# Putting a norm's token factors on all partitions: two GpSimd transfers through DRAM in place of diagonals and a product

## What is computed

```python
def _rmsnorm(x, g):
    r = lax.rsqrt(jnp.mean(xf * xf, axis=-1, keepdims=True) + EPS)
    return (xf * r).astype(x.dtype) * g

def _even_mixer(h, w_in, a_conv, b_conv, b_conv_bias, b_ln_g, b_ln_b, w_out):
    p = h @ w_in                      # 2048 -> 7168
    a_x, a_b, a_c, a_z, b_val, b_gate, b_z = jnp.split(p, 7, axis=-1)
    ya = a_b * _causal_dwconv(a_c * a_x, a_conv)          # 3 taps
    yb = b_val * jax.nn.sigmoid(b_gate)
    yb = _causal_dwconv(yb, b_conv) + b_conv_bias         # 31 taps
    yb = jax.nn.silu(_layernorm(yb, b_ln_g, b_ln_b))
    u = jnp.concatenate([ya * jax.nn.silu(a_z), yb * jax.nn.silu(b_z)], axis=-1)
    return u @ w_out

x = x + _rmsnorm(_even_mixer(_rmsnorm(x, e_norm_pre), ...), e_norm_post)
```

## Time and profile before

| | |
|---|---|
| median of 3 runs | 1347.89 us (1346.43 to 1349.7) |
| the profiled execution's own time | 1346.3 us |
| its span in the trace | 1344.5 us |
| TensorE (PE) busy | 99% of the span |
| TensorE weight loads (PEld), beside its matmuls | 82% |
| VectorE (DVE) busy | 65% |
| ScalarE (ACT) busy | 33% |
| GpSimd (POOL) busy | 7% |
| TensorE's granted clock | 0.998 of full speed |

### The profile page before, as it was taken

The page is one execution under the profiler, slowest core; times in us unless marked ns, Lnnn a source line. Parts: engine busy times, 40 slices in busy tenths (PEclk is TensorE's granted clock), DMA queues, the critical chain, the costliest instruction groups (busy, mean ns, idle before and its releaser), DMA issues.

```text
span 1344.5 us, 14691 instructions
## 1 busy us (share of the span) xinstructions
PE 1326.9 (99%) x6054; PEld 1104.8 (82%) x6054; DVE 874.3 (65%) x827; ACT 440.7 (33%) x436; POOL 96.9 (7%) x90
## 2 busy tenths in 40 slices
PE   8999999999999999999999899999999999999997
PEld 7888888888888888888888799888888888788886
DVE  6499999999846544536955984444522222499788
ACT  6421212221222121234555552222222223345452
POOL 0000000000009400000000100000000001400001
PEclk9999999999999999999999999999999999999999
DMA  9723333343368888753666554333343333364157
GB/s 319 218 63 94 102 106 105 94 125 94 102 179 274 250 258 250 251 188 107 241 258 233 163 161 125 96 95 95 100 113 94 94 94 95 125 219 157 43 208 251
DMA packets 229967, 209.50 MB, mean 156 GB/s; under 512 B 3616, under 2 KB 192160, under 8 KB 224928
## 3 DMA queue, kind: packets, MB, share of 16 engines
q1 hardware_dynamic: 225552, 203.61, 48.6%
q10 hardware_dynamic: 4368, 5.24, 1.2%
HBM read 187.87 MB, written 20.97 MB: 155 GB/s over the span
## 4 chain that ended last, share of the span: by engine, by line
PE 90%; DVE 5%; DMA 2%; ACT 1%; issue 1%; DVEq 0%; POOL 0%; SPq 0%; ACTq 0%
PE bank L705 30%; PE bank L709 30%; PE bank L707 30%; DVE w_lo L1490 1%; DMA scratch<-o_out 1%; DVE rows L1652 1%; ACT w_hi L1038 1%; DVE h_lo L1321 1%; DMA raw<-o_in 1%; DVE scratch L1522 1%; DVE rows L1569 0%; ACT junk L1190 0%; DVE scratch L1663 0%; DVE w_lo L1301 0%; DMA rows<-x_t 0%
## 5 line engine op out<-in xcount | busy, mean ns | idle before, releaser
L705 PE MATMUL bank<-h_hi,w_hi 128*128 128x512 f32 (+1 forms) x1536 | 585.6, 381 | 3.1 <-DVE w_lo L1343 1.6
L709 PE MATMUL bank<-h_hi,w_lo 128*128 128x512 f32 (+1 forms) x1536 | 584.0, 380 | 0.0
L707 PE MATMUL bank<-h_lo,w_hi 128*128 128x512 f32 (+1 forms) x1536 | 584.0, 380 | 0.0
L705 PEld LDWEIGHTS bank<-h_hi,w_hi 128*128 128x128 f32 x1536 | 288.8, 188 | 59.2 <-issue 4.0
L707 PEld LDWEIGHTS bank<-h_lo,w_hi 128*128 128x128 f32 x1536 | 288.8, 188 | 55.6 <-issue 0.7
L709 PEld LDWEIGHTS bank<-h_hi,w_lo 128*128 128x128 f32 x1536 | 288.8, 188 | 54.9
L1301 DVE TENSOR_TENSOR w_lo<-raw,w_hi 128x2048 fp32r<-128x2048 f32 x88 | 205.4, 2334 | 54.2 <-ACT w_hi L938 53.1
L1377 DVE SCALAR_TENSOR_TENSOR rows<-shifted,vecs,rows 128x512 f32<-128x512 f32 x256 | 198.8, 779 | 15.0 <-ACT rows L1000 7.6
L938 ACT ACTIVATE w_hi<-raw 128x2048 fp32r<-128x2048 f32 x88 | 167.9, 1910 | 87.3 <-PE bank L709 75.3
L705 PE MATMUL bank<-w_hi,h_hi 128*128 128x512 f32 x448 | 174.8, 390 | 0.6 <-DVE rows L1561 0.6
L709 PE MATMUL bank<-w_hi,h_lo 128*128 128x512 f32 x448 | 174.3, 389 | 0.0
(11 more groups left out here) (116 smaller groups left out, 718.3 us busy)
## 6 DMA issues: line engine op xcount, KB each, us to landing
raw<-e_in SPq DMA_DIRECT2D x52, 1024.0 KB, 5.7
raw<-o_in SPq DMA_DIRECT2D x32, 1024.0 KB, 6.1
scratch<-e_out SPq DMA_DIRECT2D x17, 1024.0 KB, 7.4
spare<-e_out SPq DMA_DIRECT2D x12, 1024.0 KB, 7.8
spare<-o_out SPq DMA_DIRECT2D x12, 1024.0 KB, 6.7
scratch<-o_out SPq DMA_DIRECT2D x10, 1024.0 KB, 5.1
e_sums<-scratch SPq DMA_DIRECT2D x8, 1024.0 KB, 5.1
spare<-e_sums SPq DMA_DIRECT2D x7, 1024.0 KB, 6.1
```

What stands on the lines that cost most here:

```text
L705: nc.tensor.matmul(dst, w[0], m[0], start=first, stop=False, skip_group_check=goes_on)
L707: nc.tensor.matmul(dst, w[0], m[1], start=False, stop=False, skip_group_check=goes_on)
L709: return nc.tensor.matmul(dst, w[1], m[0], start=False, stop=last, skip_group_check=goes_on)
```

## The change

The factors no longer pass TensorE. After each of the two powers GpSimd waits for it, writes the 128x4 tile `token_power` into a row of 512 words in DRAM (`rstd_rows[n]`, one word per token, so 512 places of 4 bytes), waits until that has landed, and reads the row back to all 128 partitions (2 KB each) straight into `x_rstd` or `ln_rstd`. VectorE waits for the second transfer where it waited for TensorE's product. Both sets of diagonals, both products of ones with diagonals and both copies from PSUM are gone; the square stays. The wait of step 1's last slab for `x_rstd_ready` goes with them, since bank 3 is not used for the factors any more.

```diff
--- before.py
+++ after.py
@@ -41,7 +41,6 @@
 KT = D // P
 QUARTER = KT // 4
 HALF = T // 2
-R_BANK = 3
 W_A = D // 2
 CB = W_A // P
 CONV_A, CONV_B = 3, 31
@@ -145,7 +144,7 @@
         scratch = sb("scratch", [P, KT * T])
         shifted_at = free_from[0]
         shifted = sb("shifted", [P, 3, PAD + T])
-        diagonals = sb("diagonals", [P, TT, P])
+        shifted_rest = sb("shifted_rest", [P, T])
         vecs = sb("vecs", [P, NVEC])
         ident = sb("ident", [P, P])
         ones = sb("ones", [P, P])
@@ -176,7 +175,6 @@
                   "b1": scratch[:, 3 * SLAB:], "b4": spare4[:, :]}
         buffers = [{**shared, "b2": spare2[n][:, :], "b3": spare3[n][:, :]} for n in range(2)]
         sum_buffer = (shared["b1"], shared["b4"])
-        ln_diagonals = scratch[:, 6 * T:7 * T].rearrange("p (t c) -> p t c", t=TT)
         gain_post = (shared["b1"], shared["c0"])
         gain_next = shared["c2"]
         x_resid = (shared["b0"], shared["b4"], shared["c3"], shared["b0"])
@@ -194,6 +192,8 @@
 
 
         x_mid = nc.dram_tensor("x_mid", [T, D], F32, kind="Internal").ap()
+        rstd_rows = [nc.dram_tensor(f"rstd_row{n}", [1, T], F32, kind="Internal").ap()
+                     for n in range(2)]
         e_sums = nc.dram_tensor("e_sums", [3, 4, P, SLAB], F32, kind="Internal").ap()
 
 
@@ -208,8 +208,9 @@
         x_squared = sem("x_squared")
         x_var_ready = sem("x_var_ready")
         x_power_ready = sem("x_power_ready")
-        x_spread = sem("x_spread")
         x_rstd_ready = sem("x_rstd_ready")
+        rstd_stored = sem("rstd_stored")
+        rstd_spread = sem("rstd_spread")
         sig_ready = sem("sig_ready")
         glu_ready = sem("glu_ready")
         silu_ready = sem("silu_ready")
@@ -239,7 +240,6 @@
         csum_ready = sem("csum_ready")
         vsum_ready = sem("vsum_ready")
         ln_rstd_ready = sem("ln_rstd_ready")
-        diagonals_ready = sem("diagonals_ready")
         ln_scaled = sem("ln_scaled")
         ln_silu = sem("ln_silu")
         gated = sem("gated")
@@ -295,7 +295,7 @@
         def uses4(b, part, n=0):
 
 
-            mid = 1 if b == 7 else 2
+            mid = 2 if b in (4, 5) else 1
             return {"stat": 1, "mid": mid, "map": mid + TT}[part] + n
 
         def first_bank(c):
@@ -652,6 +652,17 @@
             nc.gpsimd.tensor_tensor(token_power[:, :], token_var[:, :],
                                     minus_half[:, 0:1].to_broadcast([P, TT]),
                                     ALU.pow).then_inc(x_power_ready, 1)
+            pool.wait_ge(x_power_ready, 1)
+
+            def spread(n, dst):
+
+                pool.dma_start(rstd_rows[n].rearrange("a (t p) -> p (a t)", p=P),
+                               token_power[:, :], allow_slow_non_contiguous=True)\
+                    .then_inc(rstd_stored, 16)
+                pool.wait_ge(rstd_stored, 16 * (n + 1))
+                pool.dma_start(dst, rstd_rows[n].to_broadcast([P, T])).then_inc(rstd_spread, 16)
+
+            spread(0, x_rstd)
 
             def powers(first, count):
 
@@ -682,6 +693,8 @@
             nc.gpsimd.tensor_tensor(token_power[:, :], token_var[:, :],
                                     minus_half[:, 0:1].to_broadcast([P, TT]),
                                     ALU.pow).then_inc(ln_rstd_ready, 1)
+            pool.wait_ge(ln_rstd_ready, 1)
+            spread(1, ln_rstd)
 
             powers(MID, 2 * TT)
             pool.wait_ge(normed, 2 * TT)
@@ -716,14 +729,12 @@
             def operand(k, first=0, width=T):
                 return h_hi[:, k, first:first + width], h_lo[:, k, first:first + width]
 
-            def feature_major(step, moving, order=range(KT), used_at=None, before=None):
+            def feature_major(step, moving, order=range(KT), used_at=None):
 
                 for q in range(SLOTS):
                     pe.wait_ge(lo_ready, step * SLOTS + (q + 1))
                     pe.wait_ge(bank_free[q], step + 1)
                     for i, k in enumerate(order):
-                        if before is not None:
-                            before(q, i)
                         last = product(bank[q][:, :], weights(q, k, P), moving(k),
                                        i == 0, i == KT - 1)
                         if i == used_at and q == SLOTS - 1:
@@ -778,16 +789,7 @@
                 for k in range(KT):
                     first_product(q, k)
 
-            def x_spread_out(q, k):
-
-                if (q, k) == (0, QUARTER):
-                    pe.wait_ge(diagonals_ready, TT)
-                    nc.tensor.matmul(bank[R_BANK][:, :], ones[:, :], diagonals[:, :, :],
-                                     start=True, stop=True).then_inc(x_spread, 1)
-                elif (q, k) == (R_BANK, 0):
-                    pe.wait_ge(x_rstd_ready, 1)
-
-            feature_major(1, operand, before=x_spread_out)
+            feature_major(1, operand)
             with pe.Fori(2, E1A) as i:
                 feature_major(i, operand)
             with pe.Fori(E1A, E1A + 1) as i:
@@ -805,11 +807,6 @@
                                         ones[:, 0:1], start=True, stop=True)
             last.then_inc(stat_ready, 1)
             feature_major(E1A + E1B - 1, operand)
-            pe.wait_ge(diagonals_ready, 2 * TT)
-            pe.wait_ge(bank_free[6], uses4(6, "stat") + 1)
-            nc.tensor.matmul(bank[6][:, :], ones[:, :], ln_diagonals,
-                             start=True, stop=True)\
-                .then_inc(stat_ready, 1)
             with pe.Fori(E1A + E1B, E1 - 1) as i:
                 feature_major(i, operand)
             feature_major(E1 - 1, operand, [*range(2 * QUARTER, 3 * QUARTER),
@@ -1322,12 +1319,6 @@
                         h_halves[1][at], bank[4 + j][:, :].rearrange("p (k c) -> p k c", c=P),
                         f32(h_halves[0][at]), ALU.subtract).then_inc(bank_free[4 + j], 1)
 
-            def make_diagonals(dst):
-                for t in range(TT):
-                    nc.vector.tensor_scalar(dst[:, t, :], ident[:, :],
-                                            token_power[:, t:t + 1], None, ALU.mult)\
-                        .then_inc(diagonals_ready, 1)
-
             def x_rest(k):
 
                 dve.wait_ge(x_hi_ready, k + 1)
@@ -1359,12 +1350,9 @@
             nc.vector.tensor_scalar(token_var[:, :], x_sums[:, :], 1.0 / D, EPS,
                                     ALU.mult, ALU.add).then_inc(x_var_ready, 1)
             split_ahead(0, 2)
-            dve.wait_ge(x_power_ready, 1)
             dve.wait_ge(consts_set, 6)
-            make_diagonals(diagonals)
             split_ahead(0, 3)
-            dve.wait_ge(x_spread, 1)
-            link(nc.vector.tensor_copy(x_rstd, bank[R_BANK][:, :]))
+            dve.wait_ge(rstd_spread, 16)
             nc.vector.tensor_tensor(x_rstd2, x_rstd, x_rstd, ALU.mult).then_inc(x_rstd_ready, 1)
             dve.wait_ge(x_rstd_ready, 1)
 
@@ -1465,15 +1453,10 @@
                         dve.wait_ge(stat_ready, 2)
                         nc.vector.tensor_scalar(token_var[:, :], bank[5][:, 0:TT], 1.0 / W_A, EPS,
                                                 ALU.mult, ALU.add).then_inc(bank_free[5], 1)
-                    if i == E1B - 1 and q == 1:
-                        dve.wait_ge(ln_rstd_ready, 1)
-                        make_diagonals(ln_diagonals)
             finish(CB - 1, (CB - 1) % 2, tile(CB - 1))
 
 
-            dve.wait_ge(stat_ready, 3)
-            nc.vector.tensor_copy(ln_rstd, bank[6][:, :]).then_inc(bank_free[6], 1)
-            dve.wait_ge(bank_free[6], uses4(6, "stat") + 2)
+            dve.wait_ge(rstd_spread, 32)
 
             def a_low(layer, slot, first, src, n):
 
```

## The result

| | before | changed |
|---|---|---|
| median of the runs | 1347.62 us (1346.43 to 1349.7) | 1358.45 us (1356.96 to 1358.95) |
| the profiled execution | 1346.3 us, span 1344.5 us | 1358.83 us, span 1357.0 us |
| TensorE's granted clock over the span | 0.998 | 0.993 |

The ratio is 1.008 [1.0068, 1.0092]: 10.8 us slower, where 1348.1 us was forecast and 1352.0 us was the end of the range. The profiled execution of before was 1.3 us faster than its median, that of the changed kernel is 0.4 us slower than its own, so the two traces differ by 12.5 us and the medians by 10.8 us.

A forecast was written before the change was run, and what follows sets the result against it. TensorE was taken to bound the kernel, busy 1326.9 of 1344.5 us. Two products gone and one stall, -0.86 - 0.86 + 1.97 = +0.25 us, on the median 1347.89 us gave 1348.1 us; range 1345.4 to 1352.0 us.

The forecast's parts named there:

- VectorE moves as one piece: From the square at 57.65 us into step 2, VectorE's whole stretch was to shift with the square's start.
- the layer norm's pair is free: Layer norm's two transfers: even at 15.66 us the factor comes 28 us before it is wanted, so the wait costs nothing.
- The price of the delay: TensorE stalls by as much as the square starts after 57.86 us; forecast start 59.83 us, stall 1.97 us.
- the prediction's rooms: VectorE's lead over TensorE: 1.77 us at step 1's last slab, 1.07 us at step 2's second, before 0.86 us comes off.
- the price of the store: First norm's store from GpSimd to DRAM: 1.03 us for the issue plus 3.2 us for the landing.
- the low end: First norm's two transfers at 2 x 2.4 = 4.8 us, square at 55.6 us, no stall.
- the word-wise store is dear: Rival: the first norm's store of 512 4-byte pieces lands in 6.8 us; stall 5.57 us, sum +3.85 us; chance 0.20.
- The load back: First norm's read back to all partitions: 1.03 us issue, 2.9 us landing, 0.9 us for sharing with the weights.
- the high end of the pair: First norm's two transfers at 2 x (1.03 + 6.8) = 15.66 us, square at 66.43 us, stall 8.57 us.
- The first stall: TensorE was to stall first at about 107.7 us, at step 2's second slab, some 2 us long.
- The transfers did not arrive early: Rival: first norm's transfers take at most 7.1 us, no stall; -1.72 us, 1346.2 us; chance 0.22.
- GpSimd was not held off SBUF by VectorE: Rival: VectorE's low parts delay the first norm's store descriptors by 4.96 us; sum +5.2 us, 1353.1 us; chance 0.06.

The follow-up runs named there:

- e15: The changed kernel once more, unaltered, as a second measure: 1358.95 us, ratio 1.0082 against the kernel before.
- e2: The changed kernel with only the first norm's factor through DRAM, the layer norm's by diagonals and product as before: 1360.2 us, ratio 1.0086 against the kernel before.
- e4: The changed kernel with the first norm's two transfers issued by ScalarE on its own queue, same 512 words: 1357.88 us, ratio 1.0071 against the kernel before.
- e6: The changed kernel with the two weight loads beside the transfers held until the first norm's factors have landed: 1355.77 us, ratio 1.0057 against the kernel before.
- e16: The changed kernel with 32 matmuls of no use in TensorE's stall: 1359.02 us, ratio 1.0077 against the kernel before.
- e9: The changed kernel with 36 matmuls of no use in TensorE's stall: 1357.56 us, ratio 1.0078 against the kernel before.
- e10: The changed kernel with two tokens side by side per partition, stores in 256 pieces of 8 bytes: 1352.75 us, ratio 1.004 against the kernel before.
- e3: The changed kernel with each partition's four factors adjacent in DRAM, stores in 128 pieces of 16 bytes: 1348.95 us, ratio 1.0002 against the kernel before.
- e17: The changed kernel with 16-byte pieces and two held weight loads for the first norm, single words for the layer norm: 1346.36 us, ratio 0.9985 against the kernel before.
- e13: The kernel before plus an unread store of 512 pieces of 8 bytes; it and two like runs, once each: 1346.49 to 1348.43 us beside 1348.6 us.
- e7: The changed kernel with 16-byte pieces in both norms and the two weight loads held: 1347.46 us, ratio 0.9996 against the kernel before.
- e11: The kernel before with only the layer norm's factor through DRAM, in 16-byte pieces: 1346.8 us, ratio 0.9995.

## Why the prediction was wrong

**What held.** The frame of the argument held: TensorE bounds the kernel, 1.72 us of products go, nothing but the delay of the square can reach it, VectorE moves as one piece, the layer norm's pair is free, GpSimd's waiting harms nobody. The price of the delay holds too, though the agreement of its total is in part luck: 69.49 - 57.86 = 11.63 us, and the stall is 11.57 us. By the prediction's rooms the last slab of step 1, with 1.77 - 0.86 = 0.91 us of room, would have stalled for 69.49 - 57.65 - 0.91 = 10.93 us and the second slab of step 2 for the remaining 0.70 us. Measured were 0.6 us more at the first, because TensorE's first product had begun 0.6 us sooner, and nothing at the second, because the slow clock had put TensorE behind. Across all kernels in which TensorE stalled at the first of these slabs, its start follows the square by the same time, which makes the delay of the square the cause and not a neighbour of it:

| kernel | square, us | slab starts, us | difference | slab to sum, us | clock 90 to 96 us |
|---|---|---|---|---|---|
| changed | 69.49 | 96.93 | 27.44 | 318.47 | 0.50 |
| `e15` | 69.35 | 96.79 | 27.44 | 317.25 | 0.50 |
| `e2` | 69.88 | 97.32 | 27.44 | 317.61 | 0.57 |
| `e4` | 68.14 | 95.59 | 27.45 | 318.55 | 0.60 |
| `e6` | 66.24 | 93.69 | 27.45 | 318.09 | 0.64 |
| `e16` | 71.01 | 98.45 | 27.44 | 317.63 | 0.95, then 0.50 |
| `e9` | 68.07 | 95.54 | 27.47 | 316.58 | 1.00 |
| `e10` | 63.41 | 90.86 | 27.45 | 318.27 | 0.50 |
| `e3` | 61.31 | 88.77 | 27.46 | 316.53 | 1.00 |
| `e17` | 59.13 | 86.59 | 27.46 | 316.52 | 1.00 |

**The step that failed: the price of the store.** I took 1.03 + 3.2 us, from GpSimd's power and the landing of `x_mid`. It cost 0.30 us to the issue and 9.56 us from there to the landing, 9.86 us in place of 4.23 us. The row was right in direction and wrong in kind: `x_mid` is moved in long pieces, and the price of this store hangs on its pieces of 4 bytes (`e3`, `e10`, `e13`). I had named these words as what speaks against the low end, and then left them out of the sum. They were weighed only in the rival "the word-wise store is dear". That rival was the right one in sign and in the transfer that it blamed, and its marks came as written: a square beyond 62.3 us, a stall over 4.4 us, a store over 6 us, and an issue on GpSimd that was short. Its reason, a price for each of the 512 pieces, was right in part only: 512 pieces of 8 bytes took 4.6 us (`e13`). And it was priced at 6.8 us, from a transfer of 256 KB, and so ended at +3.85 us.

**The load back** was taken at 4.8 us with its issue, and took 0.29 + 7.61 us. I had let it meet a little of the weights' traffic. But the weights' loads, held up while the store ran, moved at the same time as it: from 64 to 72 us the DMA engines are busy to 0.92. With the weights held it took 5.13 us (`e6`), in `e7`, with the fours as well, some 3.6 us (from its issue at 54.10 us to the square). So each transfer exceeded its own term, and the high end of the pair, 15.66 us, was passed as well: 17.8 us. The square came 69.49 - 59.83 = 9.66 us later than forecast; 5.63 us of it are the store, 3.1 us the load back, and 0.93 us come from GpSimd's power, which ended later in this execution (51.70 us for 50.77 us).

**The first stall came earlier than I said**, at the last slab of step 1 and not at the second of step 2. The smaller room decides only while the delay is small: there the first to be late is the slab that is reached first, whose room of 0.9 us was far exceeded. The text named this as a sign of a room misread; it was not one, the rooms were right and the delay was larger than they. It should have expected the stall there even in its own forecast: a square at 59.83 us is 2.18 us late, more than 0.91 us. With a small delay both places show, as in `e3` (0.63 us at 88.77 us, 0.41 us at 111.24 us). The total is the same either way.

**A term that was missing: the clock.** A stall was priced at its own length. In the changed kernel 2.9 us come on top of it, 2.74 us of them in the 15 matmuls in which the granted clock was at 0.50 and came back. The last two columns of the table: where the clock fell, the stretch from that slab to the sum takes 317.25 to 318.55 us, 1.7 to 3.0 us more than the 315.56 us of before; where it stayed at 1.00, 1.0 us more, of which 0.41 us are the second small stall (0.42 us in `e9`). The fall itself so makes a difference of 0.7 to 2.0 us. In `e15`, the same kernel, only 7 matmuls ran slow, and the stretch takes 317.25 us in place of 318.47 us.

**The other rivals.** The transfers did not arrive early. The estimate from the Trainium skill's "DMA: Bandwidth & Descriptors", section "Anatomy of one DMA — SWDGE (gpsimd) path", 4.6 us for the pair, is far below the 17.8 us measured and also below the 6.7 us of `e7`, from issue to square; the measurement decides. The Trainium skill, same page, section "Rules for kernel authors", has a non-contiguous last dimension carried as one descriptor per element. That pointed the right way, but the number of pieces is not what the runs show to matter most (`e13`). GpSimd was not held off SBUF by VectorE: its issue took 0.94 us beside a low part of VectorE, and the square on GpSimd of the earlier trace rows has no counterpart in it.

**What stays open.** Why writes of 4 bytes are slow, and why they stop the traffic of another queue, the traces don't show: they show only that the DMA engines are idle meanwhile. The layer norm's store took 15.6 us and not 9.6 us (12.3 to 15.6 us over the kernels that have it in words), which no run explains.

## What to carry to other kernels

Price a small transfer by the size of its pieces and not by its bytes: lay the data out so that a partition's words are adjacent in DRAM, and if that can't be, put the transfer where nobody waits for it, and where no other queue's load is due either. Before a wait is put in the place of a product, set its price against the smallest room of all who follow; a stall of TensorE in which the clock falls costs more than its length, here 1.7 to 3.0 us. Moving 1.72 us off the busiest engine is worth 1.72 us at best, so the chain that takes its place has to fit its room in full.

## What the runs showed of the hardware

- A store of 2 KB from SBUF to DRAM took 8.8 to 10.7 us in 512 words of 4 bytes at about 50 us (12.3 to 15.6 us in the layer norm), 8.2 us with the four words of a partition side by side, 8.8 us as 256 words (1 KB), 4.6 us as 512 pieces of 8 bytes (4 KB), 3.3 us as 256 of 8 bytes and 1.9 to 3.7 us as 128 of 16 bytes. In the layer norm the last two took 8.4 us (`e10`) and 6.9 us (`e3`, `e11`), so something else counts as well, which no run here separates.
- It holds up others: two loads of 1 MB from SP's queue landed after 14.2 to 15.8 us in place of 6 us, and one of SP's issues lasted 7.14 us in place of 0.38 us. It does so when ScalarE issues it too: 13.1 to 14.7 us (`e4`).
- A weight load into TensorE of a 128x128 operand whose elements lie 16 bytes apart took 329 ns (`e7`), one with adjacent elements 192 ns (before).
- The granted clock fell to 0.50 in the 11.6 us in which TensorE stood. Its matmuls were back at full pace 5.7 us after the work began again, in a second run of the same kernel (`e15`) 3.1 us after.
